# Feed-forwards with the weights held still in five of six column groups, the high and low parts of x side by side as the moving operand

## The reference, cut to what matters

```
def rms_norm(x, g):
    y = x * rsqrt(mean(x * x, axis=-1) + EPS)
    return y * g
def swiglu(h, w_in, w_out):                      # w_in 1024 x 5632, w_out 2816 x 1024
    gate, up = split(h @ w_in, 2, axis=-1)
    return (silu(gate) * up) @ w_out
x = x + 0.5 * rms_norm(swiglu(rms_norm(x, g[0]), ff1_w_in, ff1_w_out), g[1])   # eight such
x = x + swiglu(rmsnorm(x, g), w_gate_up, w_down)                               # two such (ff3)
```

## Time and profile before

| | |
|---|---|
| time, median of 3 runs | 2994.71 us (2991.94 to 2996.36) |
| the profiled execution: its time | 2987.99 us |
| its span, first to last instruction | 2986.2 us |
| mean granted clock of TensorE | 0.999 of 2.4 GHz |
| TensorE busy | 2942.4 us, 99%, 15397 matmuls |
| VectorE busy | 1804.0 us, 60% |
| ScalarE busy | 1463.1 us, 49% |
| GpSimd busy | 68.8 us, 2% |
| transfers | 532.97 MB, mean 178 GB/s |

### The profile page before, as it was taken

How to read it: one execution, slowest core, us unless ns; L and a number is a source line. 1 busy time by engine, 2 the same in 40 slices (tenths; PEclk the granted TensorE clock), 3 DMA queues, 4 the chain that set the end, 5 groups by cost and what they waited for, 6 DMA issues and landing times.

```text
span 2986.2 us, 38358 instructions
## 1 busy us (share of the span) xinstructions
PE 2942.4 (99%) x15397; PEld 2490.7 (83%) x15397; DVE 1804.0 (60%) x2594; ACT 1463.1 (49%) x2127; POOL 68.8 (2%) x143
## 2 busy tenths in 40 slices
PE   8999999999999999999999999999999999999999
PEld 6889888888888888888888988897888889788887
DVE  5556655546655546765554665469675546977554
ACT  5455544445544444554443464354655434575542
POOL 0000000000000000000000000010000001000000
PEclk9999999999999999999999999999999999999999
DMA  6554455655555655265555635576244557625453
GB/s 229 187 202 159 162 186 188 197 183 198 190 184 190 197 184 190 100 197 190 191 184 183 224 122 190 184 205 209 104 155 150 189 182 206 213 86 179 154 186 130
DMA packets 302403, 532.97 MB, mean 178 GB/s; under 512 B 31074, under 2 KB 125204, under 8 KB 302228
## 3 DMA queue, kind: packets, MB, share of 16 engines
q1 hardware_dynamic: 288964, 511.63, 52.0%
q10 hardware_dynamic: 13264, 18.90, 1.8%
HBM read 528.33 MB, written 1.11 MB: 177 GB/s over the span
## 4 chain that ended last, share of the span: by engine, by line
PE 94%; DVE 2%; DMA 2%; ACT 1%; issue 1%; POOL 0%; ACTq 0%; SPq 0%; POOLq 0%; DVEq 0%
PE bank L742 90%; PE bank L1043 2%; PE bank L1083 1%; PE bank L823 1%; DMA sb_ring<-in_w_xq_dram 1%; DVE sb_parts L1847 1%; ACT sb_parts L1357 0%; PE bank L798 0%; PE bank L806 0%; DMA sb_ring<-in_ff_w_in_dram 0%; ACT sb_sc L1500 0%; DMA sb_ring<-in_w_in_dram 0%; DMA sb_arena<-in_norm_ffn_dram 0%; ACT sb_xn L1467 0%; DVE sb_oT_low L1968 0%
## 5 line engine op out<-in xcount | busy, mean ns | idle before, releaser
L1847 DVE TENSOR_TENSOR sb_parts<-sb_ring,sb_parts 128x2048 fp32r<-128x2048 f32 x480 | 1096.6, 2289 | 790.3 <-ACT sb_parts L1357 788.4
L742 PE MATMUL bank<-sb_parts,sb_hT_high 128*128 128x512 f32 (+1 forms) x4480 | 1371.4, 392 | 5.3 <-DVE sb_parts L1847 5.2
L1357 ACT ACTIVATE sb_parts<-sb_ring 128x2048 fp32r<-128x2048 f32 x480 | 914.9, 1914 | 818.9 <-PE bank L742 717.3
L742 PEld LDWEIGHTS bank<-sb_parts,sb_hT_high 128*128 128x128 f32 x4480 | 836.9, 188 | 183.9 <-issue 7.8
L742 PE MATMUL bank<-sb_parts,sb_hT_low 128*128 128x512 f32 (+1 forms) x2240 | 854.0, 391 | 0.0
L742 PE MATMUL bank<-sb_parts,sb_hidden_high 128*128 128x512 f32 x1760 | 543.4, 390 | 0.0
L742 PEld LDWEIGHTS bank<-sb_parts,sb_hT_low 128*128 128x128 f32 x2240 | 420.8, 188 | 88.0
L742 PEld LDWEIGHTS bank<-sb_parts,sb_hidden_high 128*128 128x128 f32 x1760 | 329.0, 188 | 67.8 <-issue 0.6
L742 PE MATMUL bank<-sb_parts,sb_hidden_low 128*128 128x512 f32 x880 | 342.5, 389 | 0.0
L742 PE MATMUL bank<-sb_hT_high,sb_parts 128*128 128x256 f32 x1408 | 254.9, 283 | 0.0
L742 PEld LDWEIGHTS bank<-sb_hT_high,sb_parts 128*128 128x128 f32 x1408 | 220.1, 192 | 0.0
(11 more groups left out here) (218 smaller groups left out, 1946.6 us busy)
## 6 DMA issues: line engine op xcount, KB each, us to landing
sb_ring<-in_ff_w_in_dram SPq DMA_DIRECT2D x160, 1024.0 KB, 5.1
sb_ring<-in_ff_w_out_dram SPq DMA_DIRECT2D x88, 1024.0 KB, 4.9
sb_ring<-in_w_gate_up_dram SPq DMA_DIRECT2D x40, 1024.0 KB, 5.1
sb_ring<-in_w_in_dram SPq DMA_DIRECT2D x38, 1024.0 KB, 5.2
sb_ring<-in_a_w_qkv_dram SPq DMA_DIRECT2D x24, 1024.0 KB, 5.1
sb_ring<-in_w_down_dram SPq DMA_DIRECT2D x22, 1024.0 KB, 4.9
sb_ring<-in_ff_w_in_dram SPq DMA_DIRECT2D x32, 512.0 KB, 4.9
sb_ring<-in_c_w_qkv_dram SPq DMA_DIRECT2D x12, 1024.0 KB, 5.0
```

The costliest lines, as they stand in the source:

```text
L742: return nc.tensor.matmul(o, lhsT, rhs, start=start, stop=stop)
L1357: nc.scalar.activation(halves(n, slice(0, filled(n))).high, ring[:, raw_in[n], 0:filled(n)], ACT.Copy) \
L1847: V.tensor_tensor(both.low, ring[:, raw_in[n], 0:filled(n)], both.high.bitcast(F32), ALU.subtract) \
```

## The change

In groups 1 to 5 the operands change places. The weights are stationary, in tiles of 128 features by 128 hidden columns; x moves. Its two parts now lie side by side in one tensor `hT_both`, so that one matmul of 512 columns multiplies the high weights with high x (left half of the bank) and low x (right half), and a second one of 256 columns adds low weights times high x to the left half. A bank holds 128 hidden columns (tile j of 4) by 256 rows, as high sum and low sum, and a kind (gate or up) of a group takes four banks: gate from YB, up from G. A chunk is 4 tiles x 4 k tiles x 2 = 32 matmuls. The hidden values come out as columns, so the turning of groups 1 to 5 is gone; that of the first 256 columns stays.

The halves are added outside: ScalarE copies the right half to `halves_f`, VectorE adds the left half (`gate_sum`, `up_sum`). For gate VectorE multiplies by the row factor, which now lies along the columns (`turned_factors`: two transposes a feed-forward, and a copy of their bank), and ScalarE takes silu. For up VectorE multiplies by silu; ScalarE writes the high part, VectorE the low part. The row factor of up isn't applied there but to the output: `turn` multiplies by it, and the squares for the norm take it as their scale; for the first 256 columns it is left out in the product of L1981 too. The order of the new steps between the calls of `ahead` is written by hand, as the diff shows (TensorE first, then ScalarE, then VectorE). One line sets `dynamic_dma_scratch_size=128`, which frees on-chip memory.

```diff
-        hT = Split(sb("hT_high", [P, KD, S], F32R), sb("hT_low", [P, KD, S], F32R))
+        hT_both = sb("hT_both", [P, 2, KD, S], F32R)
+        hT = Split(hT_both[:, 0, :, :], hT_both[:, 1, :, :])
...
+        silu_columns = prT[:, :, :].rearrange("p a (b s) -> p (a b) s", b=2)
+        halves_f = sb("halves_f", [P, 8, S])
...
             def ffn(st):
                 first_rows(st, [(st, "first", h) for h in range(2)], lambda t: (st, "up", 0, t))
+                turned_factors(st, (st, "norm"), 2)
...
-                        banks = [G.take(pe, (st, kind, g, t)) for t in range(NT)]
+                        banks = [(YB if kind == "gate" else G).take(pe, (st, kind, g, j)) for j in range(4)]
...
-                            for t in range(NT):
+                            for j in range(4):
+                                cols = slice(j * P, (j + 1) * P)
                                 for k in range(4):
-                                    ins = split_mm(banks[t][:, :], hT[:, 4 * h + k, t * P:(t + 1) * P], s[:, k, :],
-                                                   h == 0 and k == 0, h == 1 and k == 3)
+                                    kt = 4 * h + k
+                                    if kt:
+                                        mm(banks[j][:, 0:S], s.low[:, k, cols], hT.high[:, kt, :], False, False)
+                                    ins = mm(banks[j][:, :], s.high[:, k, cols], hT_both[:, :, kt, :], kt == 0, kt == KD - 1)
+                                    if kt == 0:
+                                        ins = mm(banks[j][:, 0:S], s.low[:, k, cols], hT.high[:, kt, :], False, False)
...
-                            if kind == "gate" and h == 0:
-                                turned_hidden(st, g - 1, YB)
-                wide_gemm(st[0], [(st, "out", m) for m in range(KF // 2)], (st, "y"), hidT, set_up if st == stages[0] else None,
-                          lambda: turned_hidden(st, GROUPS_F - 1, G))
+                            if g == 1 and kind == "gate" and h == 0:
+                                turned_hidden(st, 0, G)
+                wide_gemm(st[0], [(st, "out", m) for m in range(KF // 2)], (st, "y"), hidT, set_up if st == stages[0] else None)
...
+                def low_half(kind, g, j):
+                    act.wait_ge(matmul_done.sem, matmul_done.at((st, kind, g, j)))
+                    last_read = (kind, g, j - 2) if j > 1 else ("gate", g, j + 2) if kind == "up" else ("up", g - 1, j + 2)
+                    if last_read[1]:
+                        act.wait_ge(dve_read.sem, dve_read.at((st, *last_read)))
+                    copy(halves_f[:, j % 2, :], G.of((st, kind, g, j))[:, S:2 * S]).then_inc(act_read.sem, act_read.next((st, kind, g, j)))
...
+                def silu_of(g, j):
+                    act.wait_ge(dve_step.sem, dve_step.at((st, "summed gate", g, j)))
...
+                    nc.scalar.activation(silu_columns[:, j, :], halves_f[:, 2 + j % 2, :], ACT.Silu) \
+                        .then_inc(act_step.sem, act_step.next((st, "silu", g, j)))
+                def high_of(g, j):
+                    act.wait_ge(dve_step.sem, dve_step.at((st, "hidden", g, j)))
+                    copy(hidT.high[:, 4 * g - 2 + j, :], halves_f[:, 4 + j % 2, :]) \
+                        .then_inc(act_step.sem, act_step.next((st, "hid high", g, j)))
...
                 for g in range(1, GROUPS_F):
                     ahead((st, "gate", g, 0))
...
+                        low_half("up", g - 1, 0)
+                        low_half("up", g - 1, 1)
+                        high_of(g - 1, 0)
                     ahead((st, "gate", g, 1))
...
+                        low_half("up", g - 1, 2)
+                        high_of(g - 1, 1)
+                        low_half("up", g - 1, 3)
+                        high_of(g - 1, 2)
+                        high_of(g - 1, 3)
+                    ahead((st, "up", g, 0))
+                    low_half("gate", g, 0)
+                    low_half("gate", g, 1)
+                    silu_of(g, 0)
+                    low_half("gate", g, 2)
+                    silu_of(g, 1)
+                    ahead((st, "up", g, 1))
+                    low_half("gate", g, 3)
+                    silu_of(g, 2)
+                    silu_of(g, 3)
...
+                factors_in(st, halves_f[:, 6, :])
+                def gate_sum(g, j):
+                    dve.wait_ge(act_read.sem, act_read.at((st, "gate", g, j)))
+                    if (g, j) > (1, 1):
+                        dve.wait_ge(act_step.sem, act_step.at((st, "silu", *((g, j - 2) if j > 1 else (g - 1, j + 2)))))
+                    one = halves_f[:, 2 + j % 2, :]
+                    settle(dve, V.tensor_tensor(one, G.of((st, "gate", g, j))[:, 0:S], halves_f[:, j % 2, :], ALU.add),
+                           dve_read, (st, "gate", g, j))
+                    V.tensor_tensor(one, one, halves_f[:, 6, :], ALU.mult).then_inc(dve_step.sem, dve_step.next((st, "summed gate", g, j)))
+                def up_sum(g, j):
+                    dve.wait_ge(act_read.sem, act_read.at((st, "up", g, j)))
+                    one = halves_f[:, 4 + j % 2, :]
+                    settle(dve, V.tensor_tensor(one, G.of((st, "up", g, j))[:, 0:S], halves_f[:, j % 2, :], ALU.add),
+                           dve_read, (st, "up", g, j))
+                    dve.wait_ge(act_step.sem, act_step.at((st, "silu", g, j)))
+                    V.tensor_tensor(one, one, silu_columns[:, j, :], ALU.mult).then_inc(dve_step.sem, dve_step.next((st, "hidden", g, j)))
+                def low_of(g, j):
+                    dve.wait_ge(act_step.sem, act_step.at((st, "hid high", g, j)))
+                    d = hidT[:, 4 * g - 2 + j, :]
+                    ins = V.tensor_tensor(d.low, halves_f[:, 4 + j % 2, :], d.high.bitcast(F32), ALU.subtract)
+                    settle(dve, ins, dve_read, (st, "hid", g, j // 2) if j % 2 else (st, "hid part", g, j))
+                def first_sums(g):
+                    up_sum(g, 0)
+                    up_sum(g, 1)
+                    low_of(g, 0)
+                def last_sums(g):
+                    up_sum(g, 2)
+                    low_of(g, 1)
+                    up_sum(g, 3)
+                    low_of(g, 2)
+                    low_of(g, 3)
...
                 for g in range(1, GROUPS_F):
                     ahead((st, "gate", g, 0))
...
+                        first_sums(g - 1)
                     ahead((st, "gate", g, 1))
+                    if g > 1:
+                        last_sums(g - 1)
+                    ahead((st, "up", g, 0))
+                    for j in range(3):
+                        gate_sum(g, j)
+                    ahead((st, "up", g, 1))
+                    gate_sum(g, 3)
...
-        nc = bacc.Bacc("TRN2", target_bir_lowering=False, num_devices=1)
+        nc = bacc.Bacc("TRN2", target_bir_lowering=False, num_devices=1, dynamic_dma_scratch_size=128)
```

More of the change, by code:

```diff
@@ L1363, in squares_free, with squares @@
                     act.wait_ge(squared.sem, squared.count)
-            def squares(src, c, key):
+            def squares(src, c, key, factor=1.0):
                 squares_free()
-                nc.scalar.activation(junk, src, ACT.Square, accum_out=ssum[:, c:c + 1]).then_inc(squared.sem, squared.next(key))
+                nc.scalar.activation(junk, src, ACT.Square, scale=factor, accum_out=ssum[:, c:c + 1]).then_inc(squared.sem, squared.next(key))
             def norm_high(st, t):
@@ L1433, in ffn @@
+                def high_of(g, j):
+                    act.wait_ge(dve_step.sem, dve_step.at((st, "hidden", g, j)))
+                    copy(hidT.high[:, 4 * g - 2 + j, :], halves_f[:, 4 + j % 2, :]) \
+                        .then_inc(act_step.sem, act_step.next((st, "hid high", g, j)))
                 for g in range(1, GROUPS_F):
                     ahead((st, "gate", g, 0))
-                    hidden_high(st, g - 1)
-                    ahead((st, "gate", g, 1))
-                    for t in range(NT):
-                        act.wait_ge(matmul_done.sem, matmul_done.at((st, "gate", g, t)))
-                        act.wait_ge(dve_read.sem, dve_read.at((st, "up", g - 1, t)))
-                        nc.scalar.activation(silu[:, t, :], G.of((st, "gate", g, t))[:, :], ACT.Silu, scale=row_factor_of(st, t)) \
-                            .then_inc(act_read.sem, act_read.next((st, "gate", g, t)))
@@ L1443, in ffn @@
-                    for h in range(2):
-                        ahead((st, "up", g, h))
+                    if g == 1:
+                        hidden_high(st, 0)
+                    else:
+                        low_half("up", g - 1, 0)
+                        low_half("up", g - 1, 1)
+                        high_of(g - 1, 0)
+                    ahead((st, "gate", g, 1))
+                    if g > 1:
[4 more added lines that the diff above has]
+                        high_of(g - 1, 3)
@@ L1894, in times_gain @@
```

(33 more changed lines are left out.)

33 lines of the change are left out of this document (22 added, 11 removed).

## The result

After the change the median of four runs is 3069.61 us (3061.34 to 3091.68), against 2993.32 of four of the kernel before: ratio 1.0273, 95% interval 1.0239 to 1.0307. Forecast were 3055 us and 3010 to 3090, slower. The profiled execution took 3075.95 us, with a span of 3074.2 at a mean granted clock of 0.993; before it was 2986.2 at 0.999.

The account below looks back on a forecast made before the run. TensorE, 99% busy with matmuls 90% of the chain, was taken as the bound. -45.0 + 21.5 + 2.5 + 20 + 57 + 3.4 + 0.6 = +60 us on 2987.99: 3048, as median 3055 us; range 3010 to 3090.

Parts of the forecast that it names:

- the two waits: TensorE waits for bank 4's first rows (+20 us), and ahead of later ups and gates for VectorE's sums (+57 us).
- the loop: ScalarE and VectorE answering each other take 23.6 us a group against TensorE's 22.19; TensorE waits 5.7 us a feed-forward.
- The matmuls' own pace: Each matmul costs its columns plus 13.3 ns; 32 more instructions a group: 22.19 us, +0.43 a group, +21.5 in all.
- The first wait: First group's gate needs bank 4, whose first rows VectorE still reads: 2.2 us wait, +2.0 net a feed-forward, +20.
- the handoff costs 0.04: In the wait for bank 4, passing from VectorE's finished read to TensorE's start adds 0.04 us.
- The set-up: First stage's VectorE set-up, 4.0 us, stands between gate tile 3 and the next low part: +1.7 twice, +3.4 us.
- the ends of three feed-forwards: At three feed-forward ends the longer squares and products with the factor lie open: about 0.6 us in all.
- The loop hides: Rival: sums and silus start much earlier than the written order, only bank 4's wait is left: 2994 us; chance 0.08.
- Taking a bank doesn't hold TensorE: Rival: the last owner's read is no condition when a bank is taken, both waits go: 2974 us; chance 0.12.
- the free weight load: Rival: a 256-wide matmul takes its weight load's 190 ns instead of 120, group 26.7 us: 3220 us; chance 0.02.
- a longer loop: Rival: handoffs above 0.08 us or copies slower beside matmuls: above 3092 us; chance 0.06.
- the small steps of the loop: ScalarE and VectorE steps, 0.04 us less or more each: loop 22.9 or 24.5 us, total +29 to +97.

Follow-up runs that it names:

- e3: Changed kernel, each tile taking its bank when TensorE comes to it, silus, high copies and hidden low parts one chunk later: 2976.63 us, ratio 0.9972; again 2976.69, 0.9971.
- e4: Kernel before, with only a wait added: TensorE may not begin the first group's gate until VectorE has read bank 4's first rows: 3027.42 us, ratio 1.012.
- e2: Changed kernel, first group's gate banks turned, every tile of every group taking its bank right ahead of its own matmuls: 3045.45 us, ratio 1.0200.
- e6: Kernel before, with only the line dynamic_dma_scratch_size=128 added: 2999.38 us, ratio 1.0021.
- e1: Changed kernel; in the first group's gate the bank with the first rows goes to the fourth tile and is taken late: 3026.34 us, ratio 1.0136.
- e3b: Changed kernel, silus, high copies and hidden low parts one chunk later, all four banks of a kind still taken at once: 3095.78 us, ratio 1.0341.

## Why the prediction was right, and what it missed

The direction, the two waits, their places and the loop as the setter of the pace were right. Sizes, for one undisturbed feed-forward: from one norm's transposes to the next it took 330.82 to 517.59 = 186.77 us before and 342.96 to 536.54 = 193.58 after, +6.8 us; two more without a dip gave +6.8 and +7.0. The forecast has 5.6 there (-4.5 + 2.15 + 0.25 + 2.0 + 5.7). Two with a dip gave +8.6 and +8.7; one without gave +7.9, where one wait ahead of `up` was 1.2 us.

- *The loop* was right to 0.5%: 23.72 against 23.6 us. With TensorE's waits counted in, the forecast had 22.19 + 0.95 + 0.49 = 23.63 a group and 23.71 was measured: 0.4 us a feed-forward.
- *The matmuls' own pace* was too low: 13.3 ns more for every matmul gave 22.19 us a group, e3_again shows 22.52 with no wait. That is 0.76 above the 21.76 of before, not 0.43, so 38 us instead of 21.5. In the changed kernel it costs nothing, since the loop sets the pace. The waits are shorter instead: together 23.71 - 22.52 = 1.19 us a group and not 1.44, one of 0.60 by the profile ahead of `up`, and none of over 0.3 where 0.49 was forecast ahead of `gate`. The 32 matmuls more a group thus take back 38 of the 45 us that the removed transposes give, and -45 + 38 + 2.5 = -4.5, not -21. The span of e3_again is 12.4 under that of before, 3.4 of it the two dips; of the 9 that are left, half is not placed. e3 came out near the time that was expected of it (2973) although this term was too low.
- *The first wait* was mis-sized by the step "the handoff costs 0.04": the read ends at 352.21, and the first matmul starts at 352.78, 0.57 later. The wait is 2.63 where 2.2 was forecast: 0.4 us a feed-forward. In e4, with the wait ahead of two takes, the handoff is 0.05 (341.92 to 341.97); in the last feed-forward, where the bank is the third to be taken and not the first, 0.36 (2888.55 to 2888.91). That the half microsecond is the takes behind the one that waits is argued from this, not shown. A further 0.4 of the 1.2 between 5.6 and 6.8 I can't place.
- *The set-up* gave waits of 2.2 and 1.7 us ahead of two `up`s instead of 0.6: +2.7 us (forecast 3.4).
- *The clock* is the term that was missing: 18.8 us between the two profiled spans. Of these 12.0 are the fall in an attention stretch, which comes and goes with the kernel before too, and 10.2 the dips behind the new waits, less the 3.4 of before. Together: 10 x 6.8 + 2.7 + 18.8 = 89.5 us, against 88.0 measured between the spans. Forecast were 60. The 28 more are the clock's 18.8 and the 12 of the feed-forwards (1.2 each), less 0.7 for the set-up, the 0.6 forecast for the ends of three feed-forwards, for which this count has no term of its own, and 1.5 by which the sum overshoots. Between the medians of the runs it is 76.3 us, 16 over the forecast.
- *The rivals.* "The loop hides" fell with the high parts that don't wait for TensorE, and came true by hand in e3. "Taking a bank doesn't hold TensorE" fell with the fifty waits, "the free weight load" with groups of 22.52.
- *The chances.* 0.8 for slower was fair. The upper end, 3090, was passed by one run (3091.68, at a clock of 0.987), and by way of the clock, not of a longer loop. The room that the range left was meant for the small steps of the loop; that it held the clock's share as well is luck.

The Trainium skill, TensorE: Matmul & The Clock Gate, "HAM oscillation — how this bites in real kernels", says that TensorE, having waited for a transfer between two bursts of matmuls, starts the next burst at the lower clock. The traces of after, e2 and e4 agree for waits for VectorE of 2.2 to 4.7 us, with dips that cost 1.7 us or twice that, though behind the first waits in only five to seven of ten. I read TensorE's waits only as time and not as a cause of a lower clock.

Left open: why only five to seven of ten equal waits bring a dip, and what sets off the falls in attention stretches. They need no part of this change (e6); whether it makes them more frequent isn't shown.

## What to carry to other kernels

Where two in-order engines answer each other between the instructions that feed TensorE, add up that loop, not their busy time: engines busy for 53% (ScalarE) and 71% (VectorE) of a group made the pace, and putting each answer one feeding step later, at no instruction less and with late banks, hid all of it. Take a bank when its tile comes up and not for a whole group, but only with such an order; alone it gathers the lag into one long wait. And count waits of over 2 us on TensorE at 1.3 to 1.6 times their length on average (10 x 2.6 us with 8.5 us of dips in after, 10 x 4.3 with 25.6 in e2), since the clock may fall behind them.

## What the runs showed of the hardware that was not expected

- TensorE's granted clock falls to its lower level behind single waits of 2.2 us and more, at 1.7 or 3.4 us a time, though not behind each; in before it did so at waits of 1.75 and 1.81 us. In the feed-forwards it never did behind waits of 0.6 us (e1, some forty a run) or of 0.98 to 1.6 us (e3b, forty).
- In attention stretches it can fall without any long wait, for 12 us' worth at a time (e6, with waits of 0.33 us at most ahead of it), in some executions and not in others.
- How soon TensorE starts again behind the read that it waited for differs by place: 0.05 us (e4), 0.36 and 0.57 (after).
- A pair of matmuls of 512 and 256 columns at full clock takes 22.52 / 64 = 352 ns; by the pitch of chunks of one width, 226.7 and 120 ns, it would be 347.
